# Four of five inverse levels of an RWKV head pair as one hardware loop in TensorE's program

## The reference, cut to what matters

```
def step(state, inp):                      # rwkv7_scan, one token
    r_t, w_t, k_t, v_t, kk_t, a_t = inp
    sa = einsum('bhij,bhj->bhi', state, -kk_t)
    state = (state * w_t[:, :, None, :] + sa[..., None] * (kk_t * a_t)[:, :, None, :]
             + v_t[..., None] * k_t[:, :, None, :])
    y_t = einsum('bhij,bhj->bhi', state, r_t)
    return state, y_t
y = rwkv7_scan(r, decay_0, k_0, v, kk, a_0, False) + rwkv7_scan(r, decay_1, k_1, v, kk, a_1, True)
```

## Time and profile before

| | |
|---|---|
| median of 3 runs | 2342.64 us (2338.72 to 2343.28) |
| profiled execution, span | 2341.0 us; its own time outside the span is not given, the runs' median lies 1.6 us above the span |
| RWKV stage in the span | about 1358.8 to 1586.5 us |
| levels 1 to 4 of the four pairs | 26.83, 28.18, 28.12 and 27.45 us |
| PE busy | 96% of the span |

### The profile page before, as it was taken

How to read it: one execution, slowest core, us unless ns; L and a number is a source line. 1 busy time by engine, 2 the same in 40 slices (tenths; PEclk the granted TensorE clock), 3 DMA queues, 4 the chain that set the end, 5 groups by cost and what they waited for, 6 DMA issues and landing times. The chain is left out here.

```text
span 2341.0 us, 38427 instructions
## 1 busy us (share of the span) xinstructions
PE 2245.5 (96%) x16046; PEld 1743.2 (74%) x16046; DVE 1193.9 (51%) x2014; ACT 947.8 (40%) x1364; POOL 898.2 (38%) x678
## 2 busy tenths in 40 slices
PE   7999999999999999999999988878999999999997
PEld 5776777787877857777788777776666778888885
DVE  5544834334245467342343878854644657317334
ACT  5423355345353324654343433324266342222243
POOL 4342343334434404333344422222333445545543
PEclk9999999999999999999999989999999999999998
DMA  4221221222222202222233200002211232232332
GB/s 159 84 85 36 73 90 64 72 73 85 98 81 81 90 22 87 81 66 79 68 106 104 72 3 4 4 19 77 72 64 57 81 105 91 99 99 91 99 99 72
DMA packets 50568, 175.18 MB, mean 75 GB/s; under 512 B 6036, under 2 KB 7004, under 8 KB 50396
## 3 DMA queue, kind: packets, MB, share of 16 engines
q1 hardware_dynamic: 50396, 172.73, 22.5%
HBM read 170.60 MB, written 2.11 MB: 74 GB/s over the span
## 5 line engine op out<-in xcount | busy, mean ns | idle before, releaser
L349 POOL TENSOR_TENSOR w_low<-work,w_high 128x512 fp32r<-128x512 f32 x622 | 835.6, 1365 | 1245.2 <-ACT w_high L298 1245.2
L279 PE MATMUL ps<-x_high_tiles,w_high 128*128 128x512 f32 x1544 | 624.9, 405 | 17.5 <-POOL w_low L349 10.9
L298 ACT ACTIVATE w_high<-work 128x1024 fp32r<-128x1024 f32 x311 | 329.2, 1059 | 733.7 <-PE ps L279 730.3
L279 PE MATMUL ps<-x_low_tiles,w_high 128*128 128x512 f32 x1544 | 604.0, 391 | 0.8 <-DVE x_low_tiles L371 0.8
L279 PE MATMUL ps<-x_high_tiles,w_low 128*128 128x512 f32 x1544 | 603.5, 391 | 0.0
L279 PE MATMUL ps<-arena_parts,w_high 128*128 128x512 f32 x1264 | 397.6, 391 | 4.3 <-DVE arena L437 1.6
L279 PEld LDWEIGHTS ps<-x_high_tiles,w_high 128*128 128x128 f32 x1544 | 291.0, 188 | 118.4 <-issue 44.5
L279 PEld LDWEIGHTS ps<-x_low_tiles,w_high 128*128 128x128 f32 x1544 | 290.9, 188 | 64.2 <-DVE x_low_tiles L371 1.6
L279 PEld LDWEIGHTS ps<-x_high_tiles,w_low 128*128 128x128 f32 x1544 | 291.4, 189 | 63.3 <-issue 6.0
L279 PEld LDWEIGHTS ps<-arena_parts,w_high 128*128 128x128 f32 x1264 | 237.3, 188 | 56.8 <-issue 3.2
L279 PE MATMUL ps<-arena_parts,w_low 128*128 128x512 f32 x608 | 236.6, 389 | 0.0
(11 more groups left out here) (452 smaller groups left out, 2864.5 us busy)
## 6 DMA issues: line engine op xcount, KB each, us to landing
work<-w_first SPq DMA_DIRECT2D x178, 512.0 KB, 3.7
work<-w_second SPq DMA_DIRECT2D x134, 512.0 KB, 3.6
xT_sb<-xT SPq DMA_DIRECT2D x8, 256.0 KB, 6.0
outT<-arena SPq DMA_DIRECT2D x8, 256.0 KB, 2.1
arena<-distance_bias SPq DMA_DIRECT2D x4, 256.0 KB
small<-small SPq DMA_DIRECT2D x1, 815.5 KB, 4.5
arena<-consts SPq DMA_DIRECT2D x1, 544.0 KB, 3.8
base<-consts SPq DMA_DIRECT2D x1, 512.0 KB
```

The costliest lines, as they stand in the source:

```text
L279: ins = pe.matmul(out, lhsT, rhs, start=(n == 0 and k == 0 and q == 0), stop=(n == unit["granules"] - 1 and k == len(ops[i]) - 1 and q == 2))
L298: act.activation(m.wh[:, split_of(g), :], m.raw[:, raw_of(g), :], ACT.Copy).then_inc(sem["high_ready"], 1)
L349: pool.tensor_tensor(m.wl[:, split_of(g), part], m.raw[:, raw_of(g), part], m.wh[:, split_of(g), part].bitcast(F32), ALU.subtract).then_in ...
```

## The change

Levels 1 to 4 of a pair become one loop in TensorE's own program: the body stands there once and a register, `level`, counts 0 to 3. Since the work beside a level differs by level, two trees of branches in the body pick it by the counter. Level 5 is written out behind the loop as before. Since a wait in a loop can't name a total that grows, TensorE's waits on `lev_ready`, `m_ready`, `t1_copied` and `mt_ready` become waits for 1 that also take 1 away. As the counts of these semaphores no longer grow, DVE's own waits on `m_ready` and `mt_ready`, which followed its own earlier writes, are dropped. There is one loop for each of the four pairs; the programs of the other engines stay written out.

```diff
+            def take(name):
+                pe.wait_ge(sem[name], 1).then_inc(sem[name], -1)
+
+            def beside_in_loop(i, level, half):
+                with pe.If(level < 2):
+                    with pe.If(level < 1):
+                        beside(i, half)
+                    with pe.Else():
+                        beside(i, 2 + half)
+                with pe.Else():
+                    with pe.If(level < 3):
+                        beside(i, 4 + half)
+                    with pe.Else():
+                        beside(i, 6 + half)
...
-                for n in range(1, LAST + 1):
+                with pe.Fori(0, LAST - 1) as level:
                     for w in ways:
-                        pe.wait_ge(sem[f"lev_ready{w.d}"], LAST * i + n)
-                        pe.wait_ge(sem[f"m_ready{w.d}"], LAST * i + n)
+                        take(f"lev_ready{w.d}")
+                        take(f"m_ready{w.d}")
                         product(w, w.L, w.M, crossed_in=1).then_inc(sem[f"t1_ready{w.d}"], 1)
-                    beside(i, 2 * n - 2)
+                    beside_in_loop(i, level, 0)
                     for w in ways:
-                        pe.wait_ge(sem[f"t1_copied{w.d}"], LAST * i + n)
-                        pe.wait_ge(sem[f"mt_ready{w.d}"], (LAST + 1) * i + n)
-                        if n < LAST:
-                            product(w, w.MT, w.T1, crossed_out=1).then_inc(sem[f"x_ready{w.d}"], 1)
+                        take(f"t1_copied{w.d}")
+                        take(f"mt_ready{w.d}")
+                        product(w, w.MT, w.T1, crossed_out=1).then_inc(sem[f"x_ready{w.d}"], 1)
                     for w in ways:
                         transposed(w).then_inc(sem[f"xt_ready{w.d}"], 1)
-                    beside(i, 2 * n - 1)
+                    beside_in_loop(i, level, 1)
+                # level 5, written out with the same takes, without the second product
...
                 for w in ways:
-                    pe.wait_ge(sem[f"mt_ready{w.d}"], (LAST + 1) * (i + 1))
+                    take(f"mt_ready{w.d}")
...
-                            dve.wait_ge(sem[f"m_ready{w.d}"], LAST * i + n)
...
-                        dve.wait_ge(sem[f"mt_ready{w.d}"], (LAST + 1) * i + n)
```

More of the change, by code:

```diff
@@ L1958, in _ @@
                     ins.then_inc(sem[f"bv_ready{w.d}"], 1)
-                for n in range(1, LAST + 1):
+                with pe.Fori(0, LAST - 1) as level:
                     for w in ways:
-                        pe.wait_ge(sem[f"lev_ready{w.d}"], LAST * i + n)
-                        pe.wait_ge(sem[f"m_ready{w.d}"], LAST * i + n)
+                        take(f"lev_ready{w.d}")
+                        take(f"m_ready{w.d}")
                         product(w, w.L, w.M, crossed_in=1).then_inc(sem[f"t1_ready{w.d}"], 1)
-                    beside(i, 2 * n - 2)
+                    beside_in_loop(i, level, 0)
                     for w in ways:
-                        pe.wait_ge(sem[f"t1_copied{w.d}"], LAST * i + n)
-                        pe.wait_ge(sem[f"mt_ready{w.d}"], (LAST + 1) * i + n)
-                        if n < LAST:
-                            product(w, w.MT, w.T1, crossed_out=1).then_inc(sem[f"x_ready{w.d}"], 1)
+                        take(f"t1_copied{w.d}")
+                        take(f"mt_ready{w.d}")
+                        product(w, w.MT, w.T1, crossed_out=1).then_inc(sem[f"x_ready{w.d}"], 1)
                     for w in ways:
                         transposed(w).then_inc(sem[f"xt_ready{w.d}"], 1)
-                    beside(i, 2 * n - 1)
+                    beside_in_loop(i, level, 1)
                 for w in ways:
-                    pe.wait_ge(sem[f"mt_ready{w.d}"], (LAST + 1) * (i + 1))
+                    take(f"lev_ready{w.d}")
+                    take(f"m_ready{w.d}")
+                    product(w, w.L, w.M, crossed_in=1).then_inc(sem[f"t1_ready{w.d}"], 1)
+                beside(i, 2 * LAST - 2)
+                for w in ways:
+                    take(f"t1_copied{w.d}")
+                    take(f"mt_ready{w.d}")
+                for w in ways:
+                    transposed(w).then_inc(sem[f"xt_ready{w.d}"], 1)
+                beside(i, 2 * LAST - 1)
+                for w in ways:
+                    take(f"mt_ready{w.d}")
                     pe.wait_ge(sem[f"bv_copied{w.d}"], i + 1)
```

## The result

The changed kernel takes 2345.68 us (median of 20 runs) against 2341.2 us for the one before on the same chip: ratio 1.0018, 95% interval 1.0012 to 1.0025, some 4.5 us slower. The forecast was 2425, some 82 us slower, and the range 2347 to 2475. The rival "the body stays in the store" (2349) was nearer than the likeliest case. The profiled span grew from 2341.0 to 2345.0.

A forecast was written before the change was run, and what follows sets the result against it. The prediction took instruction fetching, 3.8 us per block of 256, to bound TensorE's stage. With the looped body fetched anew, 54 + 5 + 12 + 6 + 5 = +82 us on 2342.6 gave 2425 us, range 2347 to 2475.

The forecast's parts named there:

- the body stays in the store: Rival for the loop: only first iterations fetch, later fetch gaps vanish, branches show; 2349 us, chance 0.13.
- likeliest case: Each back edge in TensorE's loop fetches its blocks anew; 2425 us, own range 2397 to 2466, chance 0.70.
- What bounds the stage: In the RWKV stage, TensorE's program comes in blocks of 256 instructions, each 3.8 us after being asked for: too slow.
- Those blocks are gone: At the loop's back edge, 1.8 to 2.7 blocks back, the store no longer holds the body, so it is fetched again.
- The terms +54 and +12: Blocks fetched anew in later iterations: +6.0 us nine times in pairs 1 to 3, +3.9 three times in pair 0.
- F at a jump backwards: At the loop's back edge, a block's fetch takes F = 3.8 us, as in a straight line.
- First iterations: Each loop's first iteration fetches in order: +1.7 us in each of pairs 1 to 3, +5 together; pair 0's 0.
- Branches: The body's two trees of compares and jumps on TensorE's sequencer: 0.2 us a tree, +6; bounds 0 and +16.
- The clock: TensorE's clock may fall with over half of each iteration idle, lengthening tails: +5 us, between 0 and 10.
- `take`: Four more wait instructions a level, in blocks that wait for fetching anyway: 0; without that cover 6 us.
- DVE's waits: Dropping DVE's 72 waits for its own earlier writes costs nothing and gives nothing.
- The first rival: Body kept by TensorE: +5 first iterations, -8 fetch gaps, +10 branches, sum +7; 2349 us, chance 0.13.

The follow-up runs named there:

- experiment 3: The changed kernel with three or 13 blocks of dead matmuls, jumped over, in the loop's body: 2369.42 and 2369.87 us, ratios 1.0124 and 1.0123.
- experiment 4: The changed kernel with two, four, five or eight separately jumped pieces of dead matmuls in the loop's body: 2382.24, 2623.65, 2737.35 and 2906.53 us.
- experiment 2: The changed kernel with each tree of branches of pairs 1 to 3 set twice: 2349.5 us, 1.0029 against the kernel before.
- experiment 7: One count for each pair of waits, in the changed kernel: 2342.57 us, 1.0011; in the kernel before, written out: 2338.81 us, 0.9992.
- experiment 1: The changed kernel with the four levels written out again, keeping the waits that take and DVE's dropped waits: 2344.82 us, 1.0018.

## Why the prediction was wrong, point by point

- **What bounds the stage**: right for code written out. TensorE's program comes in blocks of 256, and where they stay the "issue" gaps of levels 2 to 4 go from 5.2 us to nil and q8 from 127 to 110, the count that the prediction gave for this case.
- **"Those blocks are gone"** is the step that failed. I took "never more than one block ahead" for the size of the store. It is only how far the fetching runs ahead. About eight blocks stay, in any places of the program (experiments 3 and 4), and the body covers two to four. The terms +54 and +12 hang on this step; levels 2 to 4 came out 1.0 us shorter in their place. The store of 128 KiB that the Trainium skill gives TensorE (Runtime: NRT & Kernel Launch, instruction fetch mechanics) is eight blocks of 16 KB, and the trace agrees; the rule of the same section by which a jump outside two pages must fetch does not hold here, and the measurement decides.
- **F at a jump backwards**: about right where it applies, 3.4 to 5.1 us once the body no longer fits.
- **First iterations**, +1.7 each in pairs 1 to 3: measured +2.0, +1.8 and +3.0. Blocks that come too late are in it, as said (the jumps of 1185 and 1772 ns), but so is the uncovered back edge, which that term had left out: +6.8 for the +5 of the sum.
- **Branches**, 0.2 a tree, +6: 0.15 a tree (experiment 2). The Trainium skill's 108 ns for a compare-and-branch (Advanced Engine Details and Errata, Control Flow Timing) lies above the 65 to 90 ns of the rows that fall through and below the 170 to 230 of most that jump; the rows decide.
- **The clock**, +5: little. TensorE kept its higher level (2.4 GHz, 1.00) in levels 2 to 4 of pairs 0 to 2 and had 0.91 in pair 3, after standing still for 1.65 and 2.22 us in the iteration before. The two loop kernels of experiment 3 took 19.17 and 19.12 us for the same levels at 1.00, where this one took 19.63, so by these it is worth about 0.5 us. In experiment 4, where TensorE stood still in each iteration, the granted clock of pairs 1 to 3 is 0.56 to 0.59.
- **`take`**, 0 because a wait for F hides it: wrong with the step above, since no wait for F is left. In the loop it costs 1.3 us in levels 2 to 4 against single counts (experiment 7), of the 6 that I gave as its price without cover. The 4.8 us of experiment 1 are its price written out, and 4.0 of them are longer fetch gaps.
- **DVE's waits**: 0, as said.
- **The first rival's sum** (+5, -8, +10 = +7) had the right mechanism. Measured: first iterations +6.8; levels 2 to 4 -1.0. In the latter 5.2 us of fetch gaps are gone, and the trees (24 of them at 0.15, 3.6) and the takes (1.3) give most of it back. These last two come from other pairs of kernels, so that their sum with the gaps, -0.3, meets the -1.0 only within what single profiles are good for.
- **What is open**: how much of the 6.8 of the first iterations is late blocks and how much the back edge (in pair 1 it is 0.9 and 1.15), and all of what made the stretches between the levels shorter. One profile of each kernel can't settle either.

## What to carry to other kernels

How far ahead a program is fetched says nothing of how much of it is kept: count the packets of the instruction queue before pricing a back edge. Here the loop saved the fetch gaps of its later iterations (5.2 us) and paid for it in the first, where everything unchosen is fetched too (+6.8), and in branches and in waits that must count down; together they came out 4.5 us slower. Where the matmuls are as short as these, first count the wait instructions: one count for two producers, and leaving out what a later event of the same engine implies, gave 0.3% in straight code, where the loop with the same waits had 0.2%. And before a difference of a few microseconds between two profiles is given to an edit, set the granted clock of each stretch beside it: one level's clock was worth 3 us here.

## What the runs showed that I had not expected

A wait that takes is a sequencer instruction of 51 ns, and there are 168 in the stage. What they cost depended on the code around them: 0.4 us a level written out (4.8 / 12, experiment 1), mostly as longer fetch gaps, and 0.1 in the loop (1.3 / 12, experiment 7). The keeping of blocks allows holes: 13 blocks of skipped code in the middle of a body change nothing from its second iteration on (79.21 us for levels 2 to 4 against 79.35). Past the limit it gives way at once: one landing more turned pair 0's levels of 6.4 us into levels of 28 (19.29 and 84.18 us for three, experiment 4).
